# Setting half of z's projection and half of the output weights between the heads of a mamba sublayer

## The reference

```python
def mamba2_mixer(h, w_in, conv_w, conv_b, dt_bias, A_log, D_skip, norm_w, w_out):
    proj = h @ w_in
    z, xbc, dt = jnp.split(proj, [MB_DI, MB_DI + MB_CONV_DIM], axis=-1)   # 2048, 3072, 32 columns
    xbc = silu(causal_conv_of_4_taps(xbc, conv_w) + conv_b)
    xs, Bm, Cm = jnp.split(xbc, ...)            # 32 heads of 64; 4 groups of 128 each for B and C
    dt = softplus(dt + dt_bias)
    ...                                         # y = (C B^T * exp(a_t - a_s) * dt) x per head
    y = y + D_skip * xs
    y = y * silu(z)
    y = y.reshape(B, S, 4, 512)
    y = y * rsqrt(mean(y * y, axis=-1) + EPS)   # over each of the 4 feature groups
    return (y.reshape(B, S, 2048) * norm_w) @ w_out
```

## Time and profile before

| | |
|---|---|
| median of 3 runs | 2711.35 us (2708.73 to 2712.02) |
| the profiled execution's time | 2709.46 us |
| its span, first to last instruction | 2707.7 us |
| mean granted clock of TensorE | 0.889 of 2.4 GHz |
| TensorE busy | 2273.6 us, 84% |
| VectorE, ScalarE, GpSimd busy | 43%, 30%, 8% |
| transfers | 545.11 MB, 201 GB/s mean |

### The profile page before, as it was taken

How to read it: one execution, slowest core, us unless ns; L and a number is a source line. 1 busy time by engine, 2 the same in 40 slices (tenths; PEclk the granted TensorE clock), 3 DMA queues, 4 the chain that set the end, 5 groups by cost and what they waited for, 6 DMA issues and landing times.

```text
span 2707.7 us, 29136 instructions
## 1 busy us (share of the span) xinstructions
PE 2273.6 (84%) x10882; PEld 1547.6 (57%) x10882; DVE 1160.1 (43%) x1571; ACT 810.4 (30%) x1032; POOL 218.6 (8%) x251
## 2 busy tenths in 40 slices
PE   5969769997787777999589986589989989767998
PEld 4835344442665444343268865368868867535787
DVE  2444450001453544000255553355565558445555
ACT  2324220001232521000033342243333345344333
POOL 4000011111000001222100010010010010001000
PEclk9978779998897888999889986589989989858999
DMA  9566529997455744999745552045555544213553
GB/s 174 160 234 211 177 97 418 415 410 300 134 193 194 247 177 166 417 413 413 276 162 185 172 177 78 16 148 186 171 167 183 178 149 165 77 31 101 172 185 124
DMA packets 213821, 545.11 MB, mean 201 GB/s; under 512 B 25084, under 2 KB 52828, under 8 KB 188224
## 3 DMA queue, kind: packets, MB, share of 16 engines
q1 hardware_dynamic: 187456, 507.74, 52.2%
q0 software_dynamic: 18320, 22.55, 3.6%
q10 hardware_dynamic: 7920, 13.18, 1.3%
HBM read 611.92 MB, written 13.25 MB: 231 GB/s over the span
## 4 chain that ended last, share of the span: by engine, by line
issue 44%; PE 38%; DMA 6%; DVE 6%; POOL 2%; ACT 2%; DVEq 1%; POOLq 1%; ACTq 0%; SPq 0%
PE ps L1211 8%; PE ps L472 4%; PE ps L473 4%; PE ps L474 4%; PE ps L1234 4%; PE ps L1247 3%; DMA ring<-in_ada_w 2%; PE ps L926 2%; PE ps L1269 2%; DMA ring<-in_w_in 1%; PE ps L1196 1%; POOL rs L2165 1%; DMA proj<-in_w 1%; POOLq L2164 1%; PE ps L1728 1%
## 5 line engine op out<-in xcount | busy, mean ns | idle before, releaser
L450 DVE TENSOR_TENSOR w_lo<-ring,w_hi 128x2048 fp32r<-128x2048 f32 (+3 forms) x232 | 502.7, 2169 | 559.0 <-ACT w_hi L443 554.6
L443 ACT CAST w_hi<-ring 128x2048 fp32r<-128x2048 f32 (+3 forms) x232 | 419.1, 1808 | 706.7 <-PE ps L474 665.7
L472 PE MATMUL ps<-w_hi,XTh 128*128 128x512 f32 (+3 forms) x1344 | 520.4, 387 | 16.3 <-DVE w_lo L450 9.4
L473 PE MATMUL ps<-w_lo,XTh 128*128 128x512 f32 (+3 forms) x1344 | 515.4, 383 | 0.0
L474 PE MATMUL ps<-w_hi,XTl 128*128 128x512 f32 (+3 forms) x1344 | 514.5, 383 | 0.0
L472 PEld LDWEIGHTS ps<-w_hi,XTh 128*128 128x128 f32 x1344 | 259.0, 193 | 71.0 <-issue 15.4
L474 PEld LDWEIGHTS ps<-w_hi,XTl 128*128 128x128 f32 x1344 | 258.6, 192 | 50.0
L473 PEld LDWEIGHTS ps<-w_lo,XTh 128*128 128x128 f32 x1344 | 259.6, 193 | 47.2
L926 PE MATMUL ps<-ring,mid 128*32 128x512 f32 x576 | 106.3, 767 | 60.6 <-DMA ring<-in_ada_w 39.3
L472 PE MATMUL ps<-w_hi,hTh 128*128 128x512 f32 x320 | 125.0, 391 | 0.0
L474 PE MATMUL ps<-w_hi,hTl 128*128 128x512 f32 x320 | 124.6, 389 | 0.0
(11 more groups left out here) (462 smaller groups left out, 3006.0 us busy)
## 6 DMA issues: line engine op xcount, KB each, us to landing
moe_w<-in_w SPq DMA_DIRECT2D x144, 1024.0 KB
ring<-in_ffn_w SPq DMA_DIRECT2D x128, 1024.0 KB, 5.1
ring<-in_ada_w SPq DMA_DIRECT2D x72, 1024.0 KB, 6.1
proj<-in_w SPq DMA_DIRECT2D x48, 1024.0 KB
ring<-in_w_in SPq DMA_DIRECT2D x32, 948.0 KB, 5.2
ring<-in_mb_w_in SPq DMA_DIRECT2D x20, 1024.0 KB, 5.1
ring<-in_ml_w_in SPq DMA_DIRECT2D x12, 1024.0 KB, 5.2
ring<-in_w_out SPq DMA_DIRECT2D x8, 1024.0 KB, 6.6
```

What stands on the lines that cost most here:

```text
L443: nc.scalar.copy(w_hi[:, i, 0:n], ring[:, j, 0:n]).then_inc(hi_ready, 1)
L450: nc.vector.tensor_tensor(w_lo[:, i, 0:n], ring[:, j, 0:n], w_hi[:, i, 0:n].bitcast(F32), ALU.subtract).then_inc(raw_used, 1)
L472: nc.tensor.matmul(out, sh, mh, start=start, stop=False)
L473: nc.tensor.matmul(out, sh, ml, start=False, stop=False)
```

## The change

The widths of the first part end with x (`MB_X`). The 8 pieces of z and the 8 of the output weights become units 0 to 15, each of two half units (one token tile). Units 0 to 3 and both halves of 4 stand between the scores and the transposes of x; the half units of 5 to 11 follow the outputs of the pairs in `FILL`; 12 to 15 come behind the heads. The output weights are taken by groups of 512 features: a unit is a group by 512 columns, its product is complete in PSUM, and VectorE multiplies it by the root of its group and token and adds it to `Y` (`add_out`). Square sums are taken with the squares as stationary and one column of ones as moving tile, so that they come out by token; GpSimd makes the roots. y is split into high and low part in the loop, without the root. All bounds are ScalarE's. z's last two widths are transposed behind outputs 3, 4, 7 and 8, copied, and pass through one Silu at p = 9. The banks, the buffers of `xdt` and `bc` and the semaphores are laid out anew; the double drain behind `conv` becomes one.

```diff
-        def project_move(eng, t, split, tt, widths, take, depth=2, behind=None):
-            sizes = [KH * n for n in widths for _ in range(depth)][t.ahead:]
+        def project_move(eng, t, split, tt, widths, take, depth=2, behind=None, more=0):
+            sizes = ([KH * n for n in widths for _ in range(depth)] + [PIECE] * more)[t.ahead:]
...
+        FILL = {0: (5, 0), 1: (5, 1), 2: (6, 0), 3: (6, 1), 4: (7, 0), 5: (7, 1), 8: (8, 0), 9: (8, 1),
+                10: (9, 0), 11: (9, 1), 12: (10, 0), 13: (10, 1), 14: (11, 0), 15: (11, 1)}
+        SPLIT_IN = {0: 6, 2: 7, 4: 8, 6: 9, 10: 10, 12: 11, 14: 12, 16: 13}
...
-            project_sync(sp, t, A["mb_w_out_2"][0], 0, OUT)
+            for k in range(4):
+                for j in range(2):
+                    load_piece(sp, t, blocks_of(wo[k * KH * P:(k + 1) * KH * P, j * 512:(j + 1) * 512]))
...
+            def half_unit(i, tt):
+                if tt == 0:
+                    split_arrived(pe, t)
+                wh, wl = parts(t, 512)
+                if i < 8:
+                    k, bank, lhs, first, done_ = i % 2, 0, x_lhs, i % 2 == 0, i % 2 == 1
+                    if first:
+                        pe.wait_ge((proj_act, proj_dve)[tt], t.proj.at(1))
+                else:
+                    k, bank, lhs, first, done_ = (i - 8) // 2, out_banks(i), m_lhs, True, True
+                    if i == 8:
+                        pe.wait_ge((proj_act, proj_dve)[tt], t.proj.at(1))
+                    elif i == 12:
+                        pe.wait_ge(row_read, 16)
+                    else:
+                        before = i - 1 if i < 12 else i - 2
+                        pe.wait_ge(out_added, 2 * (before - 8) + tt + 1)
+                    pe.wait_ge(mt_ready, 4 * (k + 1))
+                for b in range(KH):
+                    last = product(ps[:, bank + tt, :], lhs(k * KH + b, tt), (wh[:, b, :], wl[:, b, :]),
+                                   start=(first and b == 0), stop=(done_ and b == KH - 1))
...
+            project_tensor(pe, t, x_lhs, MB_X, arrived=x_arrived, behind=behind)
+            z_first = t.proj.count
+            scores(0)
+            unit(0)
+            turn(N_CONV - 1)
+            scores(1)
+            unit(1)
+            turn_x(0)
+            unit(2)
+            turn_x(1)
+            unit(3)
+            turn_x(2)
+            half_unit(4, 0)
+            turn_x(3)
+            half_unit(4, 1)
+            for q in range(2):
+                side_free(pe, f"z{q}")
+                turn_z(q, 0, 2)
+                turn_z(q, 1, 3)
...
+            rows_of(0)
+            rows_of(1)
             for p in range(16):
-                if p < 15:
-                    row(2 * p + 2)
-                    row(2 * p + 3)
+                if p < 14:
+                    rows_of(p + 2)
                 output(p)
-                if p >= 2:
-                    square_sum(p - 2)
+                if p in (3, 4):
+                    side_free(pe, "z2" + "ab"[p - 3])
+                    turn_z(2, p - 3, 2)
+                if p in (7, 8):
+                    side_free(pe, "z3" + "ab"[p - 7])
+                    turn_z(3, p - 7, 2)
+                if p in FILL:
+                    half_unit(*FILL[p])
+                if p >= 4:
+                    square_sums(p - 4)
+            unit(12)
+            for p in range(12, 16):
+                square_sums(p)
+            for i in range(13, 16):
+                unit(i)
...
+            def square_and_high(p):
                 act.wait_ge(gated, p + 1)
                 if p >= 4:
                     act.wait_ge(sq_used, p - 3)
+                nc.scalar.activation(gated_sq[:, p % 4, :], gated_y[:, p % 4, :], ACT.Square).then_inc(sq_ready, 1)
+                nc.scalar.activation(MTh[:, p, :], gated_y[:, p % 4, :], ACT.Copy,
+                                     scale=mb_norm[:, p:p + 1]).then_inc(mt_high, 1)
...
+            for p in range(19):
                 if p < 15:
+                    bounds(p + 1)
+                    exponentials(p + 1)
+                if p in (1, 5):
+                    take_z(act, t, 2 + p // 5, 0)
+                if p in (3, 4):
+                    z_out(2, p - 3)
+                if p in (7, 8):
+                    z_out(3, p - 7)
+                if p == 9:
+                    act.wait_ge(side_used, len(SIDE))
+                    late = zT[:, 8:16, :].rearrange("p b s -> p (b s)")
+                    nc.scalar.activation(late, late, ACT.Silu).then_inc(z_ready, 1)
+                if p >= 3:
+                    square_and_high(p - 3)
+                if p in SPLIT_IN:
+                    split_next()
...
+            project_move(dve, t, split_vector, 1, MB_X, mamba_take(dve, 1), behind=behind, more=2)
+            t.first = t.piece.count
+            scores(0)
+            split_next()
+            conv(N_CONV - 1)
+            scores(1)
+            take_z(dve, t, 0, 1)
+            split_next()
+            times_dt(0)
+            split_next()
+            times_dt(1)
+            take_z(dve, t, 1, 1)
+            split_next()
+            times_dt(2)
+            times_dt(3)
...
+            def low(p):
+                dve.wait_ge(mt_high, p + 1)
+                STT(MTl[:, p, :], gated_y[:, p % 4, :], mb_norm[:, p:p + 1], MTh[:, p, :].bitcast(F32), ALU.mult,
+                    ALU.subtract).then_inc(mt_ready, 1)
...
+                dve.wait_ge(group_rooted, g + 1)
+                dst, src = Y[:, tt, j * 512:(j + 1) * 512], ps[:, out_banks(i) + tt, :]
+                if g == 0:
+                    TS(dst, src, group_root(g, tt), None, ALU.mult).then_inc(out_added, 1)
+                else:
+                    dve.wait_ge(out_added, 2 * (i - 10) + tt + 1)
+                    STT(dst, src, group_root(g, tt), dst, ALU.mult, ALU.add).then_inc(out_added, 1)
+
+            for p in range(20):
+                if p < 16:
+                    weigh(2 * p)
+                if 10 <= p <= 16 and p % 2 == 0:
+                    add_out(8 + (p - 10) // 2, 1)
+                if 1 <= p < 17:
                     skip(p - 1)
+                if p < 16:
+                    weigh(2 * p + 1)
+                if p in (8, 12, 16):
+                    reduce(p // 4 - 2)
+                if p in (2, 6):
+                    take_z(dve, t, 2 + p // 6, 1)
+                if 3 <= p < 19:
+                    gate(p - 3)
+                if p >= 4:
+                    low(p - 4)
+                if 9 <= p <= 15 and p % 2:
+                    add_out(8 + (p - 9) // 2, 0)
+                if p in SPLIT_IN:
+                    split_next()
+            split_next()
+            add_out(12, 0)
+            add_out(12, 1)
+            reduce(3)
+            split_next()
+            used(t)
+            used(t)
+            for i in range(13, 16):
+                add_out(i, 0)
+                add_out(i, 1)
+
+        def mamba_pool(pool):
+            for g in range(4):
+                at = slice(8 + 2 * g, 10 + 2 * g)
+                pool.wait_ge(sum_read, g + 1)
+                nc.gpsimd.tensor_scalar(rs[:, 0, at], small[:, 6, 2 * g:2 * g + 2], 1.0 / 512, 1e-6, ALU.mult, ALU.add)
+                pool.drain()
+                nc.gpsimd.tensor_tensor(rs[:, 2, at], rs[:, 0, at], half[:, 0:2], ALU.pow).then_inc(group_rooted, 1)
```

More of the change, by code:

```diff
@@ new lines, in half_unit @@
+            def half_unit(i, tt):
[19 more added lines that the diff above has]
+                                   start=(first and b == 0), stop=(done_ and b == KH - 1))
+                if tt == 0:
+                    last.then_inc(half_done, 1)
+                else:
+                    last.then_inc(piece_done, 1)
+                    t.add(raw=1, piece=1)
+                    if i < 8 and i % 2:
+                        t.add(proj=1)
@@ L2562, in behind, with unit @@
+            def unit(i):
+                half_unit(i, 0)
+                half_unit(i, 1)
             def behind(j):
@@ L2641, in mamba_take, with take_z @@
             return take
+        def take_z(eng, t, q, tt):
+            if q < 2:
+                eng.wait_ge(conv_turned, 5 + q)
+            elif q == 2:
+                eng.wait_ge(conv_done, MB_CB)
+            else:
+                eng.wait_ge(z_turned, 6)
+            if tt == 0:
+                eng.wait_ge(half_done, 2 * q + 2)
+                nc.scalar.copy(z_staged(q)[:, 0, :], ps[:, 0, :]).then_inc(proj_act, 1)
+            else:
+                eng.wait_ge(piece_done, t.piece.at(t.first + 2 * q + 2 + SPLIT - t.piece.count))
+                nc.vector.tensor_copy(z_staged(q)[:, 1, :], ps[:, 1, :]).then_inc(proj_dve, 1)
+            t.add(proj=1)
         def mamba_scalar(act, t):
@@ L2660, in first_tap @@
                     silu(u - 1)
-            def gate(u):
-                act.wait_ge(conv_turned, u + 1)
-                b, name = 4 * (u - 6), f"chunk{u}"
-                for k in range(2):
```

(32 more changed lines are left out.)

321 lines of the change are left out of this document (154 added, 167 removed).

## The result

The changed kernel takes 2678.6 us (median of 4 runs, 2677.16 to 2679.62) against 2710.39 us for the kernel before on the same chip (4 runs, 2708.73 to 2712.02): ratio 0.9882, 95% interval 0.9865 to 0.9899. The prediction was 2680, with 2658 to 2702 as range. The profiled run took 2679.62 us, 29.8 less than the profiled run of before.

A forecast was written before the change was run, and what follows sets the result against it. In the heads no engine is full; TensorE waits for VectorE's weigh at half clock. 52.2 + 91.3 + 28.6 = 172.1 against 205.6, -34.5 with the close, 5 us added for the clock: -29.5, so 2680 us, range 2658 to 2702.

The forecast's parts named there:

- Ahead of the heads: Part up to the first output: predicted at 53.2 us instead of 67.8, 14.5 us off.
- clock zero: Start of the prediction's count: 2283.12 in the trace before, when the last product of the x columns is done.
- The heads: Pairs of heads with 14 half units and eight splits set in: last odd output predicted 91.3 us after the exponentials.
- e: Time when the exponentials ahead of the first output are ready, predicted 52.2 us after clock zero.
- The chain: Order of steps in the heads, with weighs behind splits and add_out: 12.05 us per two pairs from p = 10.
- the signs named: Expected in the trace after: odd outputs 9 to 13 us apart, longest around p = 5, 7 and 9; clock above 0.8.
- the clock allowance: 5 us added to the sum for half clock, two half units at 2.3 us each, between nothing and 32 us.
- 84 + 12 products: Work behind the last output, half units and units 12 to 15: 28.6 us predicted, 29.2 us off.
- The close: Closing norm behind the last product: tile 0 of Y already squared, one add of 0.7 left, about 1 us off.
- The third: Rival: TensorE stays at 1.2 GHz through the heads, 131 us, whole time 2715 us; chance 0.09 slower, 0.05 within 0.2%.
- The first rival: Chains slip less than queued, TensorE alone sets the heads: 67 us instead of 91; chance 0.20 for the part up to 2668.
- run 2652: Whole time in us, no run's number: forecast if TensorE alone sets the heads at 67 us; chance 0.20 up to 2668.

The follow-up runs named there:

- warm: Changed kernel plus products nobody reads, 16 ahead of output 7 and nine each ahead of outputs 11, 13 and 15: 2675.34 us, ratio 0.9882.
- both_late: Changed kernel with VectorE's add_out behind gate and low part, and a piece's low part behind the next pair's two weighs: 2655.86 us, ratio 0.9808.
- all_outside: Changed kernel with all 14 half units out of the heads, z's ahead of them and the output weights' behind: 2674.46 us, ratio 0.9874.
- split_late: Changed kernel with VectorE's low part of a piece moved behind the two weighs of the next pair: 2656.18 us, ratio 0.9812.
- scores_early: both_zlate with VectorE's reading of the first scores ahead of chunk 4's convolution: 2656.93 us, ratio 0.9805.
- both_zlate: both_late with ScalarE's copies z_out of z's transposes one pair later: 2654.92 us, ratio 0.9803.
- z_outside: Changed kernel with only z's half units 5 to 7 moved ahead of the heads, with their transposes, copies and Silu: 2681.19 us, ratio 0.9904.

## Why the prediction was right

**Ahead of the heads.** Exponentials ready 52.2 us after clock zero, measured 51.35; first output at 53.2, measured 52.05. The stalls are the ones named: 2.92 us ahead of scores(1) (3.2 predicted), 2.00 behind times_dt(2) (2.4). Of z's work three units were moved away from there, not the 3.5 that the prediction names: 192 products before, 120 after, which is 16.9 us and not 19.7. The sum does not use that figure.

**The heads.** Ends of the odd outputs after e, predicted and measured: 9.2 and 8.5, 18.6 and 18.1, 31.5 and 31.7, 43.5 and 44.5, 53.9 and 54.3, 67.2 and 67.5, then 79.3 and 81.4, 91.3 and 95.2. The chain was read rightly: add_out and the split stand ahead of the weigh and wait. The largest idle stretches, 3.28, 4.95 and 3.00, are at outputs 5, 7 and 11, as named. Up to output 11 all is within 1 us; the two periods after it are 13.8 us each instead of 12.05. So one of the signs named was missed: the longest periods are the last three (13.2, 13.8, 13.7), above 13 us, and not those around p = 5, 7 and 9.

**The clock.** Those 1.8 us a period are what the clock allowance was for. The half units behind outputs 11, 13 and 15 begin at half clock (0.63 us a product at 2402.09) and take 4.3 to 4.5 us instead of 2.85. In warm, with the clock at 0.95, the last output ends 90.4 us after the exponentials, where the chain had 91.3. With 3.9 us in the heads (95.2 against 91.3) and 2.9 behind them (31.5 against 28.6), less 0.85 ahead, the end of the last product is 178.05 against 172.1: about 6 us for the 5 allowed. Of the 2.9 behind the heads, 1.2 are the last eight square sums, which start 11.8 us behind the last output as forecast but have no price of their own in the sum, and 1.7 the half clock of unit 13; the cold half unit behind output 15 is hidden ahead of that. (The 84 + 12 products named there are 108; the times added are those of 108.)

That the allowance fits so well is partly luck. It was put at two half units at half clock; six of the fourteen began at it (behind outputs 0, 5, 8, 11, 13 and 15) and took 8.0 us more than 2.85 each, and the chain of the weighs hid a good part. That much was a judgement, not a term worked out.

**The close.** TensorE's idle time up to the next norm is 9.32 us against 10.67 before, 1.35 off for the 1 predicted.

**The tables.** Two loads of 1.28 us and nothing beside them. "ScalarE: Activation LUTs" of the Trainium skill, section "What ACT_TABLE_LOAD costs", would have put another 1.38 us of drain at each; this trace again does not show it.

**The rivals.** The third was wrong: the heads' clock is 0.86. "TensorE: Matmul & The Clock Gate" of the Trainium skill, section "HAM oscillation", tells of a kernel in which every burst between waits for a transfer starts cold. This trace agrees only in part: in the heads half clock followed the six waits of 2.08 us and more and none of 1.36 us or less, 10 outputs of the changed kernel ran in 0.87 us, and in both_late the heads have 0.92. Without half units in the heads, though, the clock there is 0.50 throughout (all_outside). The first rival (TensorE alone sets the heads, 67 us, run 2652) is wrong for this kernel but is what split_late and both_late came near to: 75.4 and 72.1 us of heads, runs of 2656.18 and 2655.86. Its "against", the weigh behind the split in one in-order queue, was most of the difference: the split's place alone is 20.6 us.

**What the prediction had not seen.** It took the moved work as the source of the gain ("work that could lie in it"). The sum was right, but the split of it was not: all_outside shows that the rest of the change, the new chain and the norm behind the products, brings 34.3 us of stage (216.25 to 181.93), and that setting 14 half units in the heads cost 5.4 of them. Of the 34.3, the bare heads are 30.7, and what stands behind them, with the norm, 7.3; the part ahead is 5.1 longer. The parts of the new chain (rows two pairs ahead, all bounds on ScalarE) were not tried one by one. Had I priced the chain alone, the sum itself would have shown it: bare pairs of about 3 us need 16 x 3 = 48 us of heads.

## What to carry to other kernels

Work set into gaps of a latency-bound chain brings helpers along (splits, additions of results), and these stand in the in-order queues of the engines that carry the chain. Put each behind the chain's next step, not ahead of it: here moving the splits and the additions turned a fill that lost 5 us into one that gains 19 (the splits alone: one that gains 15). And price the chain without the fill as a case of its own, since only that tells what the fill is worth. Moving one read earlier in an engine's list gains nothing if the last item of the same list is what is waited for; here it joined two short waits to a long one, and the half clock behind that cost 3.5 us (scores_early).

The fastest versions, both_zlate, both_late, scores_early and split_late (0.9803 to 0.9812), can't be told apart in whole time and are 0.7 to 0.8% faster than the changed kernel.

## What the hardware did that was not expected

The clock fell at different times behind a wait. Ahead of outputs 0, 5 and 7 of the changed kernel TensorE waited 2.40, 3.28 and 4.95 us, and the output itself ran at half clock (1.54 to 1.55 us). Behind the 3.00 us wait ahead of output 11 the output still runs in 0.87 us, and the products from 1.4 us later on take 0.63 us each where they took 0.40; the windows of TensorE from the output on, and then of the half unit:

```profile
2400.73:2402.09 1.36, 1.36 (x9) 0.95 (x10) 1.36 (x4) 1.04 (x3) 0.00 (x0) 0.82 0.72 236
2402.09:2407.86 5.77, 4.84 (x18) 3.78 (x16) 2.11 (x6) 1.95 (x6) 0.00 (x0) 0.75 0.31 122
```

Waits of 2.08 and 2.45 us (ahead of outputs 13 and 15) were followed by half clock as well, the output itself taking 0.93 and 0.99 us; with waits of the same lengths in z_outside the output itself was cold (1.55 us). The wait of 2.70 us in the earlier trace rows was followed by full clock. And the wait of 2.00 us ahead of the fourth transposes of x was followed by a granted clock of 1.00 in both_zlate and of 0.67 in scores_early (the windows above), where the instructions around it are the same. So the length of the wait alone does not decide; what else does was not tried.

The moving size did not set the price of small products: four square sums with one moving column take 0.50 us at full clock (the prediction took 0.4; the next instruction starts 0.43 us after them), as long as two row products of 256 columns.
